# 14 of the 24 modulation pairs computed on GpSimd instead of TensorE, in place in their loaded chunks

## What is computed

```python
def rms_norm(x, g):
    ...
mod = silu(c) @ ada_w[l] + ada_b[l]        # 1024 -> 6 * 1024, for each of DEPTH = 2 layers
...
(nq, nkc, nvc, nks, nvs, nkw, nvw, ngate, rq, rk, rv, rg,
 fq, fk, fv, ff, mg) = jnp.split(h @ w_in, points, axis=-1)
...
merged = (gates[:, :, 0] * (o_nsa @ w_read_nsa)
          + gates[:, :, 1] * (o_ret @ w_read_ret)
          + gates[:, :, 2] * (o_fox @ w_read_fox))
return (merged @ w_out)
```

## Time and profile before

| | us |
|---|---|
| median of 3 runs | 2006.43 |
| lowest, highest | 2006.08, 2016.94 |
| the profiled execution, first to last instruction | 2005.2 |

### The profile page before, as it was taken

The page is one execution under the profiler, slowest core; times in us unless marked ns, Lnnn a source line. Parts: engine busy times, 40 slices in busy tenths (PEclk is TensorE's granted clock), DMA queues, the critical chain, the costliest instruction groups (busy, mean ns, idle before and its releaser), DMA issues.

```text
span 2005.2 us, 27891 instructions
## 1 busy us (share of the span) xinstructions
PE 1933.1 (96%) x9976; PEld 1572.7 (78%) x9976; DVE 1473.8 (73%) x1504; ACT 1157.9 (58%) x1245; POOL 92.4 (5%) x134
## 2 busy tenths in 40 slices
PE   5999999999999999998999999999999999999996
PEld 2777888789987788887787787887878878778885
DVE  2755575744566655666788888889888888888988
ACT  1554554334434545543567767767677676766773
POOL 0510100000004300000000000000000000000000
PEclk9999999999999999999899999999999999999998
DMA  9745434585556644354799999999999999999993
GB/s 325 254 168 209 170 126 168 189 315 189 189 188 211 222 155 152 106 174 141 273 358 335 340 345 356 343 343 343 337 354 351 336 341 351 348 352 330 351 359 134
DMA packets 275630, 532.97 MB, mean 266 GB/s; under 512 B 10768, under 2 KB 23392, under 8 KB 275424
## 3 DMA queue, kind: packets, MB, share of 16 engines
q1 hardware_dynamic: 275552, 531.91, 75.6%
HBM read 530.83 MB, written 1.05 MB: 265 GB/s over the span
## 4 chain that ended last, share of the span: by engine, by line
PE 90%; DVE 5%; ACT 2%; issue 1%; DVEq 1%; DMA 0%; SPq 0%; ACTq 0%
PE pA L743 18%; PE pA L744 17%; PE pA L745 17%; PE pA L748 9%; PE pO L748 7%; PE pO L743 6%; PE pO L745 6%; PE pO L744 6%; PE pT L801 4%; DVE w_lo L1852 1%; PE pT L748 1%; ACT w_hi L1435 1%; DVE win L2085 0%; DMA x<-in_x 0%; PE pT L743 0%
## 5 line engine op out<-in xcount | busy, mean ns | idle before, releaser
L1893 DVE TENSOR_TENSOR wide_lo<-raw,wide_hi 128x2048 fp32r<-128x2048 f32 x336 | 762.5, 2290 | 123.2 <-ACT wide_hi L1435 103.6
L1435 ACT ACTIVATE wide_hi<-raw 128x2048 fp32r<-128x2048 f32 x336 | 644.7, 1921 | 214.6 <-PE pO L745 119.9
L1435 ACT ACTIVATE w_hi<-raw 128x1024 fp32r<-128x1024 f32 (+1 forms) x242 | 251.3, 1045 | 341.2 <-PE pA L745 249.8
L1852 DVE TENSOR_TENSOR w_lo<-raw,w_hi 128x1024 fp32r<-128x1024 f32 (+1 forms) x242 | 294.5, 1230 | 168.7 <-ACT w_hi L1435 159.7
L743 PE MATMUL pA<-wide_hi,x_lo 128*128 128x512 f32 x896 | 359.7, 401 | 1.4 <-DVE x_lo L2435 0.6
L745 PE MATMUL pA<-wide_hi,x_hi 128*128 128x512 f32 x896 | 355.0, 396 | 0.0
L744 PE MATMUL pA<-wide_lo,x_hi 128*128 128x512 f32 x896 | 354.9, 396 | 0.0
L743 PE MATMUL pA<-w_hi,h_lo 128*128 128x512 f32 (+2 forms) x560 | 227.4, 406 | 14.8 <-DVE w_lo L1852 10.9
L745 PE MATMUL pA<-w_hi,h_hi 128*128 128x512 f32 (+2 forms) x560 | 217.9, 389 | 0.0
L744 PE MATMUL pA<-w_lo,h_hi 128*128 128x512 f32 (+2 forms) x560 | 217.8, 389 | 0.0
L743 PEld LDWEIGHTS pA<-wide_hi,x_lo 128*128 128x128 f32 x896 | 168.7, 188 | 44.4 <-issue 3.8
(11 more groups left out here) (273 smaller groups left out, 2391.1 us busy)
## 6 DMA issues: line engine op xcount, KB each, us to landing
raw<-in_moe_w SPq DMA_DIRECT2D x336, 1024.0 KB, 6.8
raw<-in_w_in SPq DMA_DIRECT2D x56, 1024.0 KB, 5.5
raw<-in_ada_w SPq DMA_DIRECT2D x48, 1024.0 KB, 6.6
raw<-in_ffn_w SPq DMA_DIRECT2D x33, 1024.0 KB, 5.2
raw<-in_w_out SPq DMA_DIRECT2D x8, 1024.0 KB, 5.0
raw<-in_cmp_k_w SPq DMA_DIRECT2D x4, 1024.0 KB, 5.9
raw<-in_cmp_v_w SPq DMA_DIRECT2D x4, 1024.0 KB, 10.6
raw<-in_w_read_nsa SPq DMA_DIRECT2D x4, 1024.0 KB, 6.1
```

What stands on the lines that cost most here:

```text
L1435: return nc.scalar.activation(dst, src, ACT.Copy)
L1852: V.tensor_tensor(w_lo[m][:, 0:n], raw[s][:, i * n:(i + 1) * n], w_hi[m][:, 0:n].bitcast(F32), ALU.subtract).then_inc(raw_done, 1)
L1893: V.tensor_tensor(wide_lo[m][:, :], raw[g][:, :], wide_hi[m][:, :].bitcast(F32), ALU.subtract).then_inc(raw_done, 2)
```

## The change

14 pairs, called POOLED, are computed by GpSimd: ten in the mixing part of layer 0 and four in that of layer 1 (PAIR_AT gives for each the slot ahead of which its chunks are loaded and the slot in which TensorE takes the result). None is left in the dense part. For a pair GpSimd multiplies each of the eight blocks of 128 x 512 by its column of `silu(c)`, in place in `raw`, adds the eight up, four for each chunk, and leaves the sum in `part`, which is the memory of `rope_t`. TensorE transposes `part` in four blocks of 128, and VectorE sums each block over its 128 columns and then adds the bias. GpSimd frees each chunk by `pool_used` and starts the next pair, or the next rotation, once TensorE has transposed the last `part`. ScalarE has no copy to `acc` for these pairs. The ten other pairs stay as they were.

```diff
-KEPT = [(0, 2, 3, 4, 5, 6), (0, 2, 4, 6)]
+PAIR_AT = [((16, 25), (28, 32), (32, 36), (36, 41), (46, 51), (53, 57), (57, 61), (61, 66), (66, 71), (71, 77)),
+           ((30, 36), (56, 61), (62, 67), (68, 74))]
+PAIRS_BEFORE = [(1, 3, 1), (0, 1, 0)]
 
 
 def kept(l):
 
-    seen, out = {"d": -1, "s": -1}, []
-    for subs, kind, which, i in SLOTS:
-        left = []
-        for sub, c in subs:
-            if sub in seen:
-                seen[sub] += 1
-                if seen[sub] not in KEPT[l]:
-                    continue
-            left.append((sub, c))
+    out = []
+    for n, (subs, kind, which, i) in enumerate(SLOTS):
+        left = [(sub, c) for sub, c in subs if sub not in ("d", "s")]
+        if any(n == at for _, at in PAIR_AT[l]):
+            left.append(("s", 0))
+        if any(n == at for at, _ in PAIR_AT[l]):
+            left.append(("d", 0))
...
-BEHIND_DENSE = [0, 2, 0, 2, 2, 2]
...
+MIXED_PAIRS = [range(FIRST, FIRST + len(PAIR_AT[0]))]
+GAPS = [MIXED_PAIRS[0].stop]
+START = GAPS[0] + 2
+MIXED_PAIRS.append(range(START + 2, START + 2 + len(PAIR_AT[1])))
+GAPS.append(MIXED_PAIRS[1].stop)
+POOLED = [n for pairs in MIXED_PAIRS for n in pairs]
...
+        part = rope_t.rearrange("p h d -> p (h d)")
...
-                    sp.wait_ge(ada_used, b.adas.index(g - RAW) + 1)
+                    n, c = divmod(b.adas.index(g - RAW), 2)
+                    if n in POOLED:
+                        sp.wait_ge(pool_used, 2 * POOLED.index(n) + c + 1)
+                    else:
+                        sp.wait_ge(ada_used, 2 * on_pe(n) + c + 1)
...
-            def ada_sum():
-
-                pe.wait_ge(O_free[b.O.slot(partials[0])], b.O.before(partials[0]) + 1)
+            def ada_turned(n):
+
+                pe.wait_ge(part_ready, POOLED.index(n) + 1)
                 pt = take_T()
                 for k in range(4):
-                    ins = mm(pt[:, k:k + 1], acc[:, k * P:(k + 1) * P], quads[:, 0:1])
+                    ins = nc.tensor.transpose(pt[:, k * P:(k + 1) * P], part[:, k * P:(k + 1) * P], ident)
                 ins.then_inc(T_full, 1)
+                marks["part", n] = b.T.n
...
+            def ada_part(n):
+
+                part_free()
+                for c in range(2):
+                    g = ADA_SLOTS[2 * n + c]
+                    pool.wait_ge(landed[g % RAW], (g // RAW + 1) * 16)
+                    ws = [raw[g % RAW][:, k * W:(k + 1) * W] for k in range(CK)]
+                    for k in range(CK):
+                        ins = pool.tensor_scalar(ws[k], ws[k], csilu[:, c * CK + k:c * CK + k + 1], None, ALU.mult)
+                    link(ins)
+                    pool.tensor_tensor(ws[0], ws[0], ws[1], ALU.add)
+                    link(pool.tensor_tensor(ws[2], ws[2], ws[3], ALU.add))
+                    if c == 0:
+                        link(pool.tensor_tensor(part[:, :], ws[0], ws[2], ALU.add))
+                    else:
+                        link(pool.tensor_tensor(ws[0], ws[0], ws[2], ALU.add))
+                        link(pool.tensor_tensor(part[:, :], part[:, :], ws[0], ALU.add))
+                    pool.drain().then_inc(pool_used, 1)
+                pool.drain().then_inc(part_ready, 1)
+                parts.append(n)
+
+            parts = []
+
+            def part_free():
+
+                if parts:
+                    pool.wait_ge(T_full, marks["part", parts[-1]])
...
+                pairs = iter(MIXED_PAIRS[l])
+                for turn in (((C_NKC, 2),), ((C_NQ, 8), (C_NKS, 2), (C_NKW, 2)), ((C_RQ, 8),)):
+                    if turn[0][0] == C_RQ:
+                        for _ in range(PAIRS_BEFORE[l][0]):
+                            ada_part(next(pairs))
+                    part_free()
...
+                for _ in range(PAIRS_BEFORE[l][1]):
+                    ada_part(next(pairs))
                 pool.wait_ge(cum_ready, l + 1)
                 pool.wait_ge(proj_ready, WBLK * l + blocks_by(C_FQ, C_FF))
                 for g in range(2):
+                    for _ in range(PAIRS_BEFORE[l][2] * g):
+                        ada_part(next(pairs))
...
+                for n in pairs:
+                    ada_part(n)
...
-            def ada_columns(l, at, n):
-
+            def ada_columns(n):
+
+                l, at = n // ADA, n % ADA * 4
                 pt, free = T_in()
-                V.tensor_tensor(mod[:, l, bass.ds(at, 4 * n)], pt[:, 0:4 * n], cols[:, l, bass.ds(at + R_ADAB, 4 * n)], ALU.add).then_inc(free, 1)
+                V.tensor_reduce(mod4[:, :], pt[:, :].rearrange("p (k n) -> p k n", k=4), AX_X, ALU.add).then_inc(free, 1)
+                dve.wait_ge(free, b.T.before(b.T.n - 1) + 1)
+                link(V.tensor_tensor(mod[:, l, at:at + 4], mod4[:, :], cols[:, l, at + R_ADAB:at + R_ADAB + 4], ALU.add))
```

More of the change, by code:

```diff
@@ L293, with on_pe, ada_slots @@
 QUAD = P // CK
[L296 to L318, removed]
+MIXED_PAIRS = [range(FIRST, FIRST + len(PAIR_AT[0]))]
[4 more added lines that the diff above has]
+POOLED = [n for pairs in MIXED_PAIRS for n in pairs]
+assert GAPS[1] + 2 == DEPTH * ADA and START == GAPS[0] + 2
+def on_pe(n):
+    return n - sum(m < n for m in POOLED)
+def ada_slots():
+    out, g = list(range(2 * EARLY)), 2 * EARLY
+    for chunk in range(2 * LAYER_CHUNKS):
+        g += 1
+        out += range(g, g + BEHIND.get(chunk, 0))
+        g += BEHIND.get(chunk, 0)
+    return out
+ADA_SLOTS = ada_slots()
 T_USES = {"k0": 1, "k2": 1, "o": 2, "s": 1}
-O_USES = {"k3": 1, "f1": 1, "d": 1}
+O_USES = {"k3": 1, "f1": 1}
 def t_uses(sub, c):
@@ L818, in gate_row @@
                     ins.then_inc(T_full if late else A_full, 1)
[L820 to L828, removed]
             def head(c0, h, t, w=HD):
@@ L1392, in _ @@
                 half = HD // 2
-                for part in (((C_NKC, 2),), ((C_NQ, 8), (C_NKS, 2), (C_NKW, 2)), ((C_RQ, 8),)):
-                    for c0, nh in part:
+                pairs = iter(MIXED_PAIRS[l])
[4 more added lines that the diff above has]
+                    part_free()
+                    for c0, nh in turn:
                         pool.wait_ge(proj_ready, WBLK * l + blocks_by(c0, c0 + nh * HD))
@@ L1518, in _ @@
             skip(b.raw, 2 * EARLY)
-            due = Due()
-            def ada_ended(first):
-                for what, n in due.after(first, b.hl.n // 2):
-                    if what == "pair":
-                        ada_copy(n)
-                    else:
-                        skip(b.T, 1)
             n_norm, n_hf, n_dev = [0], [0], [0]
@@ L1661, in first @@
                             skip(b.O, 1)
-                hi_columns(early(ADA + FIRST + 1) if l else first)
-                n_pair = FIRST if l == 0 else ADA + FIRST + 2
+                hi_columns(early(START + 1) if l else first)
                 last = None
@@ L1853, in split_to @@
                     skip(b.raw, i * BEHIND.get(h // 2, 0))
-            due = Due()
-            def ada_ended(first):
-                for what, n in due.after(first, b.hl.n // 2):
-                    if what == "pair":
-                        skip(b.O, 1)
-                    else:
-                        ada_columns(n // ADA, n % ADA * 4, 1)
-            def ada_columns(l, at, n):
+            def ada_columns(n):
+                l, at = n // ADA, n % ADA * 4
                 pt, free = T_in()
-                V.tensor_tensor(mod[:, l, bass.ds(at, 4 * n)], pt[:, 0:4 * n], cols[:, l, bass.ds(at + R_ADAB, 4 * n)], ALU.add).then_inc(free, 1)
+                V.tensor_reduce(mod4[:, :], pt[:, :].rearrange("p (k n) -> p k n", k=4), AX_X, ALU.add).then_inc(free, 1)
+                dve.wait_ge(free, b.T.before(b.T.n - 1) + 1)
+                link(V.tensor_tensor(mod[:, l, at:at + 4], mod4[:, :], cols[:, l, at + R_ADAB:at + R_ADAB + 4], ALU.add))
             def ada_columns_early(n):
@@ L2240, in first @@
                         dve.wait_ge(tab_in, 32)
-                modulate(l, 0, True, early(ADA + FIRST) if l else first)
-                n_pair = FIRST if l == 0 else ADA + FIRST + 2
+                modulate(l, 0, True, early(START) if l else first)
+                n_pair = MIXED_PAIRS[l].start
                 last = None
```

55 lines of the change are left out of this document (18 added, 37 removed).

## The result

The changed kernel takes **2113.3 us** (median, 2111.2 to 2117.1) against 2006.5 before: ratio 1.051, 95% interval 1.047 to 1.054. It is slower by 5%, and the forecast of 2001 us (1978 to 2034) is wrong, in size and in sign. The profiled execution has a span of 2114.8 us, 109.6 more than before.

A forecast was written before the change was run, and what follows sets the result against it. The prediction took TensorE, busy for 96% of the span, as the bound: 2005.2 - 33.5 removed + 28.2 of waits back = 1999.9 us for the profiled span, so a median of 2001 us, range 1978 to 2034.

The forecast's parts named there:

- What is removed, 33.5 us: On TensorE: each of 14 pairs saves 2.39 us net, a pair and a sum gone, four transposes added.
- The multiplication at 0.65 us: On GpSimd: price of one multiplication by a column, taken between a half-width copy's 0.39 us and an addition's 1.26.
- A pair of 14.6 + 0.7n: On GpSimd: us for a pair over n slots, with 0.7 us a slot for meetings with VectorE.
- Waits of TensorE, 28.2 us: Time given back: 4.0 + 6.9 + 9.3 + 3 + 4 + 1 us for waits, clock and banks.
- Slot 24 for a load: Layer 0: TensorE waits 5.4 us for a chunk of w3, counted as 4.0 since earlier idle time falls into it.
- Slot 32 for the sum: Layer 0: TensorE waits 6.9 us for the pair that GpSimd starts after its third rotation turn.
- Slots 36, 41 and 51: Layer 0: no wait, GpSimd ahead of TensorE by 5 us and more.
- That of slot 72: Layer 0: a load into the buffer of the pair taken at 71 comes late, TensorE waits 4.4 us.
- The clock, 4 us: TensorE: two new waits of 5 us and more each bring on a lower granted clock, 2 us each.
- Layer 1, 3 us: Layer 1, slots 62 to 74: waits between 0 and 6 us, including a chunk behind a pair at 68; 3 taken.
- The rival "GpSimd is the bound": Mixing parts: multiplication at 1.3 us, pair 19.8 + 0.9n, waits of 68 us, kernel slower at 2041 us; chance 0.18.
- VectorE late: Rival: GpSimd's instructions hold up `w_lo`, TensorE waits for that, layers' tails lose 5 us and more each; 2015 us; chance 0.07.

The follow-up runs named there:

- e5: Changed kernel without GpSimd's operations in the 14 pairs, and with four chunks of layer 0's first two pairs handed back ahead of the rotations; 1971.4 us.
- e1: Changed kernel without GpSimd's 15 operations in each of the 14 pairs; waits, signals, transposes and loads stay; 1990.0 us.
- e2: Changed kernel without the 8 multiplications of each pair, the 7 additions kept; 2014.1 us.
- e11: Changed kernel with the multiplication as a product with the broadcast column, over 256 of the 512 columns only; 2047.0 us.
- e3: Changed kernel with the multiplication by a column made a product of two tensors, the column read with stride 0; 2076.1 us.
- e9: Kernel before with 10 of the 24 pairs on GpSimd, multiplied by the broadcast column, their chunks placed late in the order of loads; 1996.1 us.
- e10: Changed kernel with the chunks of layer 0's first pair loaded ahead of slot 26 instead of 16, its sum at 27 instead of 25; 2092.5 us.

## Why the prediction was wrong

The runs form a ladder. Each step adds one thing, and its size holds for this order (us; each time is known to some 4 to 8 us by the intervals above): the ceiling 1971.4 (e5); chunks handed back behind the rotations 18.6 (e1); the additions and the late slots 24.1 (e2); multiplications at the predicted price 32.9 (e11); their real price 66.3 (2113.3).

- **What is removed, 33.5 us: right.** e5 leaves all of TensorE's work of the change in place and gives 1971.4 against 1972.9.
- **The dense part shorter by 11 us: right,** 10.8.
- **The multiplication at 0.65 us: the largest error, 66 us.** 1.55 where it was alone, and the upper bound of the text, 1.26, was too low as well. The bound came from the nearest row with two inputs, on the ground that one input can't cost more. It can: the same product as a tensor by a column took 1.55 and as two tensors 1.04 (36 of e3's 112 that no VectorE instruction met took 1.03 to 1.04). The row of 1.09 us in the trace before was overlooked. The row of a copy, from which the value was taken, says nothing about an arithmetic operation with a column. The Trainium skill ("GPSIMD Engine Reference", 4.1 Engine selection) says that operations with one input run roughly at line rate. The traces here do not bear that out for this form, which was the slowest of the three.
- **A pair of 14.6 + 0.7n: right in its form.** With the price of the text, e11 has 14.9 and up to 19.5. "Over 18 us: I am wrong" was met by the 25.1 us of the changed kernel.
- **Waits of TensorE, 28.2 us: too small by 46 even at the predicted pair** (2047 - 2001, e11; against the ceiling the waits are 76, table at e11). Three parts of that step failed. *Slot 24 for a load:* the list asked when the chunk would be needed by TensorE (5.4 us late), not when ScalarE would stand in front of it. ScalarE stands three slots ahead, so TensorE stopped behind slot 21's product, and once more ahead of slot 24 (7.7 us in the changed kernel, for ScalarE's `qT`). *Slot 32 for the sum:* the real stall is at slot 29, by the same route through `PT`; in the changed kernel it took 18.0 us of waiting. At slot 32 itself TensorE waited 5.1 us, near the 6.9 forecast, but by luck: the sum lay ready from 190.3 on, TensorE came at 194.8 and waited for ScalarE's `qT` behind one more late chunk. In e11 this wait was 0.8 us. *Slots 36, 41 and 51, "ahead by 5 us and more":* for the sums GpSimd was ahead at 36 (done at 225.0, taken at 237.2) and 1.1 us late at 51. But the late chunks were not looked for: slots 33, 35 and 51 of the changed kernel were 11.6, 12.5 and 12.0 us long against 3.7, 6.7 and 5.3 in e5, and with the predicted pair of e11 slots 33 and 51 still 9.8 and 7.9 (35 lost nothing there).
- **A late load was looked for at two slots only (24, 72).** That of slot 72 came as forecast, 4.4 us: slot 71 took 4.3 us more in e11 than in e5. The text treated GpSimd's pair as something that TensorE waits for at the sum. But a pair also holds two of six load buffers from their landing on, while it queues behind rotations. The measure of it is ScalarE's wait for loads in layer 0's mixing: 5.8 us in e5, 26.4 in e1, 64.4 in e2, 105.9 in e11, 161.8 in the changed kernel, in the order of their times, and none in e9. SyncE's wait is a poorer one, since e10 is 20.8 us faster with 429 of the 451 us still there.
- **The clock, 4 us: too small.** Some 30 us in layer 0's mixing by the estimate above, granted clock 0.86. It goes with the waits: over the whole span it is 0.955 in the changed kernel and 0.985 in e5.
- **Layer 1, 3 us: too small.** Two stalls, slots 66 and 73, which took 18.7 and 9.1 us instead of 3.6 and 2.8.
- **The rival "GpSimd is the bound", 2041 us,** named the right side and the right mechanism, with a chance of 0.18, and was itself 72 us short. Its pair of 19.8 + 0.9n, 23.4 to 25.2 us over four to six slots, is about the one that the changed kernel has (25.1 in the mean). So even with the right pair the waits came out too small: it too lacked the route through the ring.
- **VectorE late: the price of a meeting was right.** The mean `w_lo` of the changed kernel rose from 1.24 to 1.32 only, but the 95 of 234 that ran beside an instruction of GpSimd took 1.47 in the mean, where 1.5 was forecast, and the others 1.22. How much of the 24 us of e2 comes from such meetings and how much from chunks held was not separated; no run takes the meetings away alone. In the trace of e2 some 20 of the 24 us over e1 sit in slots 21, 22, 29, 33, 34, 71 and 72, and at 21, 29, 33 and 71 ScalarE stood still for a load, for 9.6 to 17.8 us. This speaks for the chunks; the share stays open.

## What to carry to other kernels

When work moves to a slow engine, ask first how long it holds the buffers that a prefetch ring lives on, counted from their landing and with all that stands ahead of it in that engine's queue: place each load so that the buffer is back by the slot in which the fast engine would have freed it. A late load is felt where the first in-order engine stands in front of it, here ScalarE three slots ahead of the use; "issue" as the releaser of a long wait means looking at that engine's rows. An operation that the trace doesn't show should be bounded with room above the nearest row, and the nearest row is one of the same arithmetic.

## What the hardware showed unexpectedly

- On GpSimd a multiplication of 128 x 512 fp32 by one value for each partition took 1.55 us, the sum of two tensors 1.26 and the product with a column read at stride 0 1.04 (each where VectorE left it alone; changed kernel and e3). The form with the fewest inputs was the dearest.
- Two short VectorE instructions with two inputs and one with one, of 16 elements, took 0.96 to 1.01 us beside GpSimd's products of two tensors instead of 0.17 to 0.18 (e9 and e5). So the price of a meeting does not go by the length of the VectorE instruction: it was 0.8 us for these, and 0.25 us in the mean for a `w_lo` of 1.22 us. The Trainium skill ("SBUF — State Buffer", Who interferes with whom) states an exclusive lock for a VectorE instruction with two inputs. The two rows with two inputs agree, and the row with one input was held as long.
- Fourteen pairs of additions alone, 9 to 13 us each on GpSimd (e2), in place of 2.4 us each on TensorE, change the time by nothing that can be measured.
